# Block-ordered attention steps in a transformer kernel: division at the outputs, weight halves apart, turned q and k through SBUF

## The chip, the cores and the metric

The kernel runs on one core of a Trainium2 chip. The metric is the time of one execution in device microseconds. Three runs of the kernel before gave 3099.89, 3100.74 and 3101.68 us.

## The reference, cut to what matters

The program is two transformer blocks of width 1,024 over 1,024 tokens. The change touches the token mixer of one layer of the second, a "forgetting" attention with 16 heads of 64:

```python
def fox_mixer(h, w_in, b_f, q_g, k_g, w_out):
    proj = h @ w_in
    q, k, v, f_pre = jnp.split(proj, [D, 2 * D, 3 * D], axis=-1)
    q = rms_norm_2(q.reshape(B, S, N_HEADS_2, HEAD_DIM_2), q_g)
    k = rms_norm_2(k.reshape(B, S, N_HEADS_2, HEAD_DIM_2), k_g)
...
    F = jnp.cumsum(log_f, axis=1).transpose(0, 2, 1)
...
        logits = (jnp.einsum('bqhd,bkhd->bhqk', q_i, k).astype(jnp.float32) * scale
                  + (F_i[..., :, None] - F[..., None, :]))
        logits = jnp.where(k_pos[None, :] <= q_pos[:, None], logits, -jnp.inf)
        p = jax.nn.softmax(logits, axis=-1).astype(v.dtype)
        return jnp.einsum('bhqk,bkhd->bqhd', p, v)
...
    return o @ w_out
```

Everything is float32. The kernel splits each operand into a high part in fp32r and the rest, and multiplies high by high, high by low and low by high.

## The kernel before

`attention` works on heads in 8 pairs. For a pair, eight token tiles of 128 are projected: for each tile, 8 slices of k with three matmuls each (`split_mm`, L1622 to L1624) into bank 4. ACT takes q and k out as rows (`rows_out`, L2064) and v in high and low (L2065, with DVE's `v_low`, L2151). Two tiles make a batch: ACT squares, DVE sums (`sums`, L2157), POOL takes the root (`root`, L1907), DVE multiplies (`normed`, L2162), TensorE turns q and k into bank 5 or 6 (`turn_batch`, L2003), and from there ACT writes the high parts (`high_batch`, L2081 to L2083: q once and k twice, for each head) and DVE the low ones (`low_batch`, L2171 and L2173).

A group is 256 query rows of one head, so a pair has 8 groups (4 a head, g = 0 to 3), and a group has g + 1 blocks of 256 keys. For a group: TensorE makes two tiles of logits in banks 0 to 3 (`logits`, L1958 to L1960), DVE adds the forget sums (`forgotten`, L2130), ACT takes the exponential and its row sum (`exp`, L2039), POOL takes the reciprocal and scales the whole rows (`share`, L1912 and L1914), TensorE turns them block by block into bank 5 or 6 (`turn_probs`, L1975), ACT rounds to the high part (`high_probs`, L2048), DVE subtracts (`low_probs`, L2137), and TensorE weighs v (`weigh`, L1991 and L1992) into one half of bank 7. The result has two terms on different partitions: ACT copies one (`copy_out`, L2056) and DVE adds the other (`add_out`, L2144) into `outT`, which is one tile stored per pair by SyncE (L1888).

Every engine's order is written out by hand over slots, one slot for a group. Slot n holds the logits of group n + 1, the turning and weighing of group n, and one whole tile of the next pair's projections, broken up between them. Eight slots ahead of the first group hold the projections of pair 0. `w_qkv` holds half of a pair's weights; a half is loaded by three DMAs (L1864) once DVE has subtracted the one before it (`high_weights`, L2034, and `low_weights`, L2118, both halves in a pair's last slot).

## Time and profile before

| what | value |
| --- | --- |
| median of three runs | 3100.74 us |
| the profiled execution | 3103.1 us, its span 3101.4 us |
| TensorE matmul busy | 2564.8 us, 83% |
| DVE, ACT, POOL busy | 60%, 40%, 18% |
| the stage of the change | from 1548.8 to 2251 us in the span |

Busy shares are over the whole program; the stage of the change is some 702 us of it. A matmul's duration is longer than the distance to the next one's start, since matmuls overlap. Plain rows of a view name the line, the engine, what is written and read, the shape and the count.

### The profile page before, as it was taken

The page shows a single profiled execution, that of the slowest core. Times are in us where ns is not written, and L with a number is a line of the kernel's source. Part 1 is how long each engine was busy: PE and PEld are TensorE (multiplying, and loading weights), DVE is VectorE, ACT ScalarE, POOL GpSimd, SP SyncE. Part 2 cuts the span into 40 slices and gives each one's busy share as a digit, 9 for nine tenths or more (in the row PEclk, how much of TensorE's full clock was granted, in tenths as well). Part 3 has the DMA queues.
Part 4 walks back from the last instruction along what each step waited for, and adds up shares of the span by engine and source line. Part 5 has one row for each costly group of instructions (what it writes and reads, how often), then busy time and mean ns, then how long its engine had stood idle before and what let it go on. Part 6 is the DMA issues. An engine that isn't in the chain of part 4 may idle for free. (4 is left out here: it accounts for less than half of the span.)

```text
span 3101.4 us, 34604 instructions
## 1 busy us (share of the span) xinstructions
PE 2564.8 (83%) x12069; PEld 2116.0 (68%) x12069; DVE 1848.8 (60%) x2460; ACT 1250.9 (40%) x1817; POOL 563.9 (18%) x609
## 2 busy tenths in 40 slices
PE   3998767556999999981478888888685999999999
PEld 2766456455887888870377777777564888888887
DVE  6873693355888888875435555555445445554554
ACT  2212531105777777772245555555422121112111
POOL 1000020111111111104225555555400000000000
PEclk8999758757999999995599999999796999999999
DMA  5683233417968799985111110110042111111111
GB/s 210 220 291 111 96 122 102 158 42 304 393 269 318 289 390 399 398 326 217 55 52 42 41 35 31 41 31 32 7 176 68 41 54 54 41 54 41 54 54 55
DMA packets 137677, 443.01 MB, mean 143 GB/s; under 512 B 15134, under 2 KB 74050, under 8 KB 124264
## 3 DMA queue, kind: packets, MB, share of 16 engines
q1 hardware_dynamic: 124140, 394.97, 34.7%
q0 software_dynamic: 8144, 27.80, 2.5%
q10 hardware_dynamic: 5292, 18.94, 1.5%
q8 instruction: 58, 0.95, 0.1%
q14 instruction: 43, 0.35, 0.0%
HBM read 384.91 MB, written 56.76 MB: 142 GB/s over the span
## 5 line engine op out<-in xcount | busy, mean ns | idle before, releaser
L1622 PE MATMUL psum<-w_high,block_hT_high 128*128 128x512 f32 x576 | 233.4, 405 | 22.8 <-DVE w_low L1328 18.0
L2428 DVE TENSOR_TENSOR x<-x,psum 128x512 f32<-128x512 f32 x256 | 172.8, 685 | 112.4 <-PE psum L1624 112.4
L1622 PE MATMUL psum<-w_qkv_high,fox_hT_high 128*128 128x384 f32 x512 | 199.8, 390 | 34.5 <-DVE w_qkv_low L2118 25.0
L1623 PE MATMUL psum<-w_low,block_hT_high 128*128 128x512 f32 x576 | 226.7, 393 | 0.0
L1624 PE MATMUL psum<-w_high,block_hT_low 128*128 128x512 f32 x576 | 226.4, 393 | 0.0
L1328 DVE TENSOR_TENSOR w_low<-w_up,w_high 128x2048 fp32r<-128x2048 f32 x72 | 161.7, 2288 | 90.0 <-ACT w_high L1322 90.0
L1622 PE MATMUL psum<-hT_high,w_mlp_in_high 128*128 128x512 f32 x512 | 200.1, 391 | 7.1 <-DVE w_mlp_in_low L2405 7.1
L1623 PE MATMUL psum<-hT_low,w_mlp_in_high 128*128 128x512 f32 x512 | 199.9, 390 | 0.0
L1624 PE MATMUL psum<-hT_high,w_mlp_in_low 128*128 128x512 f32 x512 | 199.7, 390 | 0.0
L1622 PE MATMUL psum<-w_mlp_out_high,hiddenT_high 128*128 128x512 f32 x512 | 199.2, 389 | 0.0
L1623 PE MATMUL psum<-w_mlp_out_low,hiddenT_high 128*128 128x512 f32 x512 | 199.2, 389 | 0.0
L1624 PE MATMUL psum<-w_mlp_out_high,hiddenT_low 128*128 128x512 f32 x512 | 199.2, 389 | 0.0
L1328 DVE TENSOR_TENSOR w_low<-w_gate,w_high 128x2048 fp32r<-128x2048 f32 x72 | 164.3, 2284 | 40.0 <-ACT w_high L1322 39.9
L2137 DVE TENSOR_TENSOR probsT_low<-psum,probsT_high 128x512 fp32r<-128x512 f32 (+1 forms) x160 | 98.9, 634 | 135.6 <-ACT probsT_high L2048 135.0
L1623 PE MATMUL psum<-w_qkv_low,fox_hT_high 128*128 128x384 f32 x512 | 176.8, 345 | 0.0
L1624 PE MATMUL psum<-w_qkv_high,fox_hT_low 128*128 128x384 f32 x512 | 176.6, 345 | 0.0
L1322 ACT ACTIVATE w_high<-w_gate 128x2048 fp32r<-128x2048 f32 x72 | 137.5, 1913 | 91.9 <-DMA w_gate<-in_w_expert_gate 84.2
L1991 PE MATMUL psum<-probsT_high,v_high_low 128*128 128x256 f32 x320 | 96.6, 321 | 81.1 <-DVE probsT_low L2137 80.7
L1328 DVE TENSOR_TENSOR w_low<-w_down,w_high 128x2048 fp32r<-128x2048 f32 x72 | 161.5, 2282 | 3.5 <-ACT w_high L1322 3.5
L2416 DVE TENSOR_TENSOR relu_squared<-relu 128x512 f32<-128x512 f32 x64 | 44.2, 691 | 194.2 <-ACT relu L2384 194.2
L2379 ACT ACTIVATE w_mlp_out_high<-w_mlp_out 128x2048 fp32r<-128x2048 f32 x16 | 30.7, 1917 | 319.0 <-DVE w_mlp_out L2409 319.0
L1622 PEld LDWEIGHTS psum<-w_high,block_hT_high 128*128 128x128 f32 x576 | 109.7, 190 | 58.9 <-DVE w_low L1328 32.5
(402 smaller groups left out, 6704.7 us busy)
## 6 DMA issues: line engine op xcount, KB each, us to landing
w_gate<-in_w_expert_gate SPq DMA_DIRECT2D x32, 2048.0 KB
w_up<-in_w_expert_up SPq DMA_DIRECT2D x32, 2048.0 KB, 9.1
w_down<-in_w_expert_down SPq DMA_DIRECT2D x32, 2048.0 KB, 10.4
v_aug<-in_w_ada SPq DMA_DIRECT2D x48, 512.0 KB, 4.8
expert_rows<-block_out ACTq DMA_DIRECT2D x36, 512.0 KB, 9.1
v_aug<-in_ada_w SPq DMA_DIRECT2D x32, 512.0 KB, 4.7
expert_rows<-work SPq DMA_DIRECT2D x1, 16384.0 KB, 44.1
w_mlp_in<-in_w_mlp_in SPq DMA_DIRECT2D x16, 1024.0 KB, 5.1
```

The source lines that it names most:

```text
L1322: act.activation(wh[:, par, half], raw[kind][:, half], ACT.Copy).then_inc(s_wh, 1)
L1328: dve.tensor_tensor(wl[:, par, half], raw[kind][:, half], wh[:, par, half].bitcast(F32), ALU.subtract).then_inc(s_wl, 1)
L1622: pe.matmul(out, sh, mh, start=start, stop=False)
L1623: pe.matmul(out, sh, ml, start=False, stop=False)
L1624: return pe.matmul(out, sl, mh, start=False, stop=stop)
L1991: pe.matmul(out_, v, pTh[:, y % 2, at], start=s == 0, stop=False)
L2137: dve.tensor_tensor(pTl[:, y % 2, 0:width], bank[5 + z % 2][:, 0:width], pTh[:, y % 2, 0:width].bitcast(F32), ALU.subtract).then_inc(s_lo, 1)
L2379: act.activation(w2h[:], w2[:], ACT.Copy).then_inc(s_w2h, 1)
L2416: dve.tensor_tensor(gf[:, g % 2, :], rl[:, g % 2, :], rl[:, g % 2, :], ALU.mult).then_inc(s_sq, 1)
L2428: dve.tensor_tensor(x3[:, t, at], x3[:, t, at], bank[4 + j % 4], ALU.add).then_inc(s_r, 1)
```

## The change

The slots become steps, 20 to a pair, one for each block. Step y turns block y + 1 and weighs block y; a group's logits stand four steps ahead of its first block. The 64 slices of the next pair's projections are dealt to the first 18 steps of a pair (`parts`), and none to the last two. POOL no longer scales the rows: it scales the columns of a diagonal by the reciprocals, a plain f32 matmul of `ones` with it spreads them over the partitions into the second half of bank 7, and DVE multiplies the outputs by that. Bank 7 then holds one group. The two weight halves are rounded at steps 17 and 19 of a pair. Turned q and k are copied by ACT with their gain into the tile of the squares in SBUF; POOL copies the high parts from there, ACT copies k across the partitions, and DVE subtracts in SBUF. The probabilities have a buffer for each g.

```diff
             F = sbuf(c2, "forget_sums", [P, 2, S])
-            pe_ = sbuf(c2, "probs_even", [P, 5 * P + 6 * P])
-            po_ = sbuf(c2, "probs_odd", [P, 7 * P + 8 * P])
+            pb = [sbuf(c2, f"probs{g}", [P, (4 * g + 3) * P]) for g in range(4)]
             pTh = sbuf(c2, "probsT_high", [P, 2, HALF], F32R)
             pTl = sbuf(c2, "probsT_low", [P, 2, HALF], F32R)
             o = sbuf(c2, "outT", [P, S])
+            dg = sbuf(c2, "recip_diagonal", [P, 2, 2 * P])
...
+            STEPS = 20
+            AHEAD = 4
+            BUSY = 18
+            parts = ((0, 4, 8), (0, 4, 8), (0, 3, 6, 8), (0, 4, 8), (0, 4, 8), (0, 3, 6, 8), (0, 4, 8), (0, 4, 8))
+            shares = [(t, range(a_, b_)) for t in range(TT) for a_, b_ in zip(parts[t], parts[t][1:])]
+            blocks = [(n, b) for n in range(NG) for b in range(n % QUADS + 1)]
...
+            def group_at(y):
+
+                n, b = blocks[y + AHEAD] if 0 <= y + AHEAD < NY else (None, 1)
+                return n if b == 0 else None
+
+            def left_at(y):
+
+                n, b = blocks[y - 1] if y >= 1 else (None, None)
+                return n if n is not None and b == n % QUADS else None
+
+            def products_at(y):
+
+                i, c = y // STEPS + 1, y % STEPS
+                if i >= PAIRS or c >= BUSY:
+                    return []
+                t, ks = shares[c]
+                return [(TT * i + t, k) for k in ks]
+
+            def tile_at(y):
+
+                done = [q for q, k in products_at(y) if k == KT - 1]
+                return done[0] if done else None
+
+            def batch_at(y):
+
+                q = tile_at(y) if y >= -STEPS else None
+                return q // 2 if q is not None and q % 2 == 1 else None
+
+            z_block, z_batch = {}, {}
+            for y in steps:
+                if 0 <= y + 1 < NY:
+                    z_block[blocks[y + 1]] = len(z_block) + len(z_batch)
+                if batch_at(y - 2) is not None:
+                    z_batch[batch_at(y - 2)] = len(z_block) + len(z_batch)
+
+            holds = {z: ("block", y_block[nb]) for nb, z in z_block.items()} | {z: ("batch", m) for m, z in z_batch.items()}
...
-                        pool.tensor_scalar(probs(n, u), probs(n, u), rs[:, j % 4:j % 4 + 1], None, ALU.mult).then_inc(s_p, 1)
-
-                    for n in slots:
-                        if batch_in(n) is not None:
-                            root(batch_in(n))
-                        if 0 <= n + 1 < NG:
+                        if n >= 2 and u == 0:
+                            pool.wait_ge(s_rb, n - 1)
+                        pool.tensor_scalar(dg[:, n % 2, u * P:(u + 1) * P], ident[:], rs[:, j % 8:j % 8 + 1], None, ALU.mult).then_inc(s_dg, 1)
+
+                    def high_batch(m):
+                        i, c = divmod(m, 4)
+                        at = slice(2 * c * P, 2 * (c + 1) * P)
+                        pool.wait_ge(s_bs, m + 1)
+                        pool.wait_ge(s_rq, m + 1)
+                        for h in range(2):
+                            pool.tensor_copy(qs[rows[h], i % 2, h, at], sq[rows[h], 0, :])
+                            ins = pool.tensor_copy(kh[rows[h], i % 2, h, at], sq[rows[h], 1, :])
+                        ins.then_inc(s_bh, 1)
+                        pool.wait_ge(s_bh, m + 1)
+
+                    shared = 0
+                    for y in steps:
+                        if batch_at(y - 3) is not None:
+                            if shared:
+                                pool.wait_ge(s_dg, 2 * shared)
+                            high_batch(batch_at(y - 3))
+                        if batch_at(y - 1) is not None:
+                            root(batch_at(y - 1))
+                        if group_at(y - 1) is not None:
                             for u in range(2):
-                                share(2 * (n + 1) + u)
+                                share(2 * group_at(y - 1) + u)
+                            shared += 1
...
+                    def bank_left(z):
+
+                        if z >= 2:
+                            kind, at = holds[z - 2]
+                            if kind == "block":
+                                pe.wait_ge(s_lo, at + 1)
+                            else:
+                                pe.wait_ge(s_bs, at + 1)
+
...
-                            pe.wait_ge(s_p, 2 * n + 2)
+                            pe.wait_ge(s_ex, 2 * n + 2)
...
-                        half = (n % 2) * 2 * P
-                        if b == 0 and n >= 2:
-                            pe.wait_ge(s_o, n - 1)
-                        pe.wait_ge(s_lo, z_block[n, b] + 1)
+                        if b == 0 and n >= 1:
+                            pe.wait_ge(s_o, n)
+                        pe.wait_ge(s_lo, y + 1)
                         for s in (2 * b, 2 * b + 1):
                             v = va[:, i % 2, s, 2 * DH * h:2 * DH * (h + 1)]
                             if s <= 2 * g:
-                                out_, at = bank[7][:, half:half + 2 * P], slice((s % 2) * 2 * P, (s % 2 + 1) * 2 * P)
+                                out_, at = bank[7][:, 0:2 * P], slice((s % 2) * 2 * P, (s % 2 + 1) * 2 * P)
                             else:
-                                out_, at = bank[7][:, half + P:half + 2 * P], slice(2 * P, 3 * P)
+                                out_, at = bank[7][:, P:2 * P], slice(2 * P, 3 * P)
                             pe.matmul(out_, v, pTh[:, y % 2, at], start=s == 0, stop=False)
                             ins = pe.matmul(out_, v, pTl[:, y % 2, at], start=False, stop=s == 2 * g + 1)
                         ins.then_inc(s_pv, 1)
+                        if b == g:
+                            pe.wait_ge(s_dg, 2 * n + 2)
+                            pe.matmul(bank[7][:, 2 * P:HALF], ones[:], dg[:, n % 2, :], start=True, stop=True).then_inc(s_rb, 1)
 
...
-                    for n in slots:
-                        logits(n + 1, 0)
-                        project(n, (0, 1))
-                        logits(n + 1, 1)
-                        project(n, (2, 3))
-                        if n >= 0:
-                            g = n % QUADS
-                            turn_probs(n, 0)
-                            project(n, (4,))
-                            for b in range(g + 1):
-                                if b < g:
-                                    turn_probs(n, b + 1)
-                                    project(n, (5 + b,))
-                                elif g < 3:
-                                    project(n, range(5 + g, KT))
-                                weigh(n, b)
-                        else:
-                            project(n, range(4, KT))
-                        if batch_in(n) is not None:
-                            turn_batch(batch_in(n))
+                    for y in steps:
+                        if 0 <= y + 1 < NY:
+                            turn_probs(*blocks[y + 1])
+                        if group_at(y) is not None:
+                            logits(group_at(y), 0)
+                            logits(group_at(y), 1)
+                        for q, k in products_at(y):
+                            project(q, k)
+                        if y >= 0:
+                            weigh(*blocks[y])
+                        if batch_at(y - 2) is not None:
+                            turn_batch(batch_at(y - 2))
...
-                        act.wait_ge(s_pv, y_block[n, g] + 1)
+                        act.wait_ge(s_rb, n + 1)
                         if g == 0 and h == 0 and i >= 1:
                             act.wait_ge(s_st, 16 * i)
-                        half = (n % 2) * 2 * P
-                        act.activation(o[rows[h], 2 * g * P:2 * (g + 1) * P], bank[7][rows[1 - h], half:half + 2 * P], ACT.Copy).then_inc(s_oc, 1)
-
-                    def rows_out(n):
-                        q = n + TT
+                        act.activation(o[rows[h], 2 * g * P:2 * (g + 1) * P], bank[7][rows[1 - h], 0:2 * P], ACT.Copy).then_inc(s_oc, 1)
+
...
                         act.wait_ge(s_raw, 2 * m + 2)
                         if m >= 1:
-                            act.wait_ge(s_ss, m)
+                            act.wait_ge(s_bh, m)
+                            act.wait_ge(s_bx, m)
+                            act.wait_ge(s_bl, m)
                         act.activation(sq[:], qk[:, 2 * (m % 2):2 * (m % 2) + 2, :], ACT.Square).then_inc(s_sq, 1)
 
...
+                    def stage_batch(m):
+                        z = z_batch[m]
+                        act.wait_ge(s_t, z + 1)
+                        act.wait_ge(s_ss, m + 1)
+                        for x, gain in ((0, gq[:, 2:3]), (1, gq[:, 1:2])):
+                            ins = act.activation(sq[:, x, :], bank[5 + z % 2][:, 2 * x * P:2 * (x + 1) * P], ACT.Copy, scale=gain)
+                        ins.then_inc(s_bs, 1)
                         i, c = divmod(m, 4)
-                        z = z_batch[m]
                         at = slice(2 * c * P, 2 * (c + 1) * P)
-                        src = bank[5 + z % 2]
-                        act.wait_ge(s_t, z + 1)
+                        act.wait_ge(s_bs, m + 1)
                         for h in range(2):
-                            act.activation(qs[rows[h], i % 2, h, at], src[rows[h], 0:2 * P], ACT.Copy, scale=gq[rows[h], 2:3])
-                            act.activation(kh[rows[h], i % 2, h, at], src[rows[h], 2 * P:HALF], ACT.Copy, scale=gq[rows[h], 1:2])
-                            ins = act.activation(kh[rows[1 - h], i % 2, h, at], src[rows[h], 2 * P:HALF], ACT.Copy, scale=gq[rows[h], 1:2])
-                        ins.then_inc(s_hi, 1)
+                            ins = act.activation(kh[rows[1 - h], i % 2, h, at], sq[rows[h], 1, :], ACT.Copy)
+                        ins.then_inc(s_bx, 1)
...
+                    for y in steps:
+                        if 0 <= y + 1 < NY:
+                            high_probs(*blocks[y + 1])
+                        if left_at(y) is not None:
+                            copy_out(left_at(y))
+                        if group_at(y - 1) is not None:
+                            exp(2 * group_at(y - 1))
+                            exp(2 * group_at(y - 1) + 1)
+                        if batch_at(y - 3) is not None:
+                            stage_batch(batch_at(y - 3))
+                        if y % STEPS == BUSY - 1 and y // STEPS + 2 < PAIRS:
+                            high_weights(2 * (y // STEPS + 2))
+                        if tile_at(y) is not None:
+                            rows_out(tile_at(y))
+                        if batch_at(y) is not None:
+                            square(batch_at(y))
+                        if y % STEPS == STEPS - 1 and y // STEPS + 2 < PAIRS:
+                            high_weights(2 * (y // STEPS + 2) + 1)
...
                         dve.wait_ge(s_oc, n + 1)
-                        dve.tensor_tensor(o[rows[h], at], o[rows[h], at], bank[7][rows[h], half:half + 2 * P], ALU.add).then_inc(s_o, 1)
-
-                    def v_low(n):
-                        q = n + TT
+                        dve.tensor_tensor(o[rows[h], at], o[rows[h], at], bank[7][rows[h], 0:2 * P], ALU.add).then_inc(s_oa, 1)
+                        dve.wait_ge(s_oa, n + 1)
+                        dve.tensor_tensor(o[rows[h], at], o[rows[h], at], bank[7][rows[h], 2 * P:HALF], ALU.mult).then_inc(s_o, 1)
...
-                        z = z_batch[m]
                         at = slice(2 * c * P, 2 * (c + 1) * P)
-                        src = bank[5 + z % 2]
-                        dve.wait_ge(s_hi, z + 1)
+                        dve.wait_ge(s_bh, m + 1)
                         for h in range(2):
-                            dve.scalar_tensor_tensor(qs[rows[1 - h], i % 2, h, at], src[rows[h], 0:2 * P], gq[rows[h], 2:3],
-                                                     qs[rows[h], i % 2, h, at].bitcast(F32), ALU.mult, ALU.subtract)
-                            ins = dve.scalar_tensor_tensor(kl[rows[h], i % 2, h, at], src[rows[h], 2 * P:HALF], gq[rows[h], 1:2],
-                                                           kh[rows[h], i % 2, h, at].bitcast(F32), ALU.mult, ALU.subtract)
-                        ins.then_inc(s_lo, 1)
+                            dve.tensor_tensor(qs[rows[1 - h], i % 2, h, at], sq[rows[h], 0, :], qs[rows[h], i % 2, h, at].bitcast(F32), ALU.subtract)
+                            ins = dve.tensor_tensor(kl[rows[h], i % 2, h, at], sq[rows[h], 1, :], kh[rows[h], i % 2, h, at].bitcast(F32), ALU.subtract)
+                        ins.then_inc(s_bl, 1)
...
+                    for y in steps:
+                        if 0 <= y + 1 < NY:
+                            low_probs(*blocks[y + 1])
+                        if left_at(y) is not None:
+                            add_out(left_at(y))
+                        if batch_at(y - 2) is not None:
+                            normed(batch_at(y - 2))
+                        if group_at(y) is not None:
+                            forgotten(2 * group_at(y))
+                            forgotten(2 * group_at(y) + 1)
+                        if batch_at(y - 1) is not None:
+                            sums(batch_at(y - 1))
+                        if batch_at(y - 4) is not None:
+                            low_batch(batch_at(y - 4))
+                        if y % STEPS == BUSY - 1 and y // STEPS + 2 < PAIRS:
+                            low_weights(2 * (y // STEPS + 2))
+                        if tile_at(y) is not None:
+                            v_low(tile_at(y))
+                        if y % STEPS == STEPS - 1 and y // STEPS + 2 < PAIRS:
+                            low_weights(2 * (y // STEPS + 2) + 1)
```

## Rows read from the trace of the kernel before

**Rows 1.** The page's first line.

```profile
span 3101.4 us, 34604 instructions
```

**Rows 2.** Timeline of SyncE's DMA issues: start, duration, line, name, count.

```profile
1693.24 0.50 SPq L1888 DMA_DIRECT2D heads_outputs<-outT  x1
...
2102.43 0.34 SPq L1888 DMA_DIRECT2D heads_outputs<-outT  x1
...
2181.64 69.33 SPq L1888 DMA_DIRECT2D heads_outputs<-outT  x2
```

**Rows 3.** Windows: busy of PE, PEld, DVE, ACT, POOL; granted clock, DMA share, GB/s.

```profile
1857.00:1940.00 83.00, 70.54 (x434) 62.36 (x433) 46.24 (x99) 46.86 (x109) 44.08 (x41) 0.98 0.13 40
2189.00:2251.00 62.00, 41.02 (x189) 32.98 (x187) 25.70 (x53) 23.89 (x52) 30.15 (x24) 0.69 0.00 1
```

**Rows 4.** Waits from 1560 to 2252: total us, times, longest.

```profile
PE psum L1991 <- DVE probsT_low L2137: 80.7, 68, 2.8
```

**Rows 5.** Timeline of TensorE in a middle pair.

```profile
1873.00 0.39 PE L1958 MATMUL psum<-k_high_twice,q_stacked 128*128 128x512 f32 x1
...
1873.96 0.42 PE L1622 MATMUL psum<-w_qkv_high,fox_hT_high 128*128 128x384 f32 x1
...
1874.57 0.33 PE L1622 MATMUL psum<-w_qkv_high,fox_hT_high 128*128 128x384 f32 x1
...
1875.09 0.60 PE L1975 MATMUL psum<-ident,probs_even 128*128 128x128 f32 x4
1875.45 0.42 PE L1622 MATMUL psum<-w_qkv_high,fox_hT_high 128*128 128x384 f32 x1
```

**Rows 6.** Timeline of TensorE, plain f32 matmuls of 512 columns.

```profile
320.46 1.88 PE L549 MATMUL psum<-ucT,wq 128*128 128x512 f32 x4
322.18 1.88 PE L549 MATMUL psum<-ucT,wk 128*128 128x512 f32 x4
```

**Rows 7.** Groups of instructions, 1560 to 2252, shapes kept apart.

```profile
L2137 DVE TENSOR_TENSOR probsT_low<-psum,probsT_high 128x512 fp32r<-128x512 f32 x96 | 64.7, 687 | 77.4 <-ACT probsT_high L2048 77.0
...
L2048 ACT ACTIVATE probsT_high<-psum 128x512 fp32r<-128x512 f32 x96 | 55.0, 589 | 29.6 <-PE psum L1975 29.4
L1907 POOL TENSOR_TENSOR qk_sums<-qk_sums,minus_half 128x8 f32<-128x8 f32 x32 | 53.6, 1674 | 2.7
L1914 POOL TENSOR_SCALAR probs_odd<-probs_odd,row_sum 128x1024 f32<-128x1024 f32 x16 | 45.7, 2854 | 1.6
...
L2171 DVE SCALAR_TENSOR_TENSOR q_stacked<-psum,qk_gain,q_stacked 64x256 fp32r<-64x256 f32 x64 | 30.9, 483 | 48.6 <-ACT k_high_twice L2083 48.2
...
L2081 ACT ACTIVATE q_stacked<-psum,qk_gain 64x256 fp32r<-64x256 f32 x64 | 30.1, 470 | 18.8 <-PE psum L2003 17.5
...
L2144 DVE TENSOR_TENSOR outT<-outT,psum 64x256 f32<-64x256 f32 x64 | 26.7, 417 | 4.1 <-ACT outT L2056 3.2
...
L2056 ACT ACTIVATE outT<-psum 64x256 f32<-64x256 f32 x64 | 24.1, 376 | 19.1 <-PE psum L1992 18.6
...
L2039 ACT ACTIVATE probs_odd<-probs_odd,row_min 128x1024 f32<-128x1024 f32 x16 | 18.4, 1150 | 30.4 <-DVE row_min L2130 30.4
...
L1914 POOL TENSOR_SCALAR probs_even<-probs_even,row_sum 128x256 f32<-128x256 f32 x16 | 14.9, 934 | 1.6
...
L1914 POOL TENSOR_SCALAR probs_even<-probs_even,row_sum 128x128 f32<-128x128 f32 x16 | 9.8, 614 | 1.6
```

**Rows 8.** Timeline of all engines, second weight half of the next pair.

```profile
1600.70 1.76 DVE L2118 TENSOR_TENSOR w_qkv_low<-w_qkv,w_qkv_high 128x1536 fp32r<-128x1536 f32 x1 [1.21 <-ACT w_qkv_high L2034]
...
1604.56 0.66 PE L1622 MATMUL psum<-w_qkv_high,fox_hT_high 128*128 128x384 f32 x1 [3.94 <-DVE v_high_low L2151]
...
1607.51 1.48 ACT L2034 ACTIVATE w_qkv_high<-w_qkv 128x1536 fp32r<-128x1536 f32 x1 [2.85 <-DMA w_qkv<-in_fox_w_in]
```

**Rows 9.** DMA issues, 1540 to 2260: KB each, median us from issue to landing.

```profile
heads_outputs<-outT SPq DMA_DIRECT2D x8, 512.0 KB, 4.8
```

More of the change, by code:

```diff
@@ L2038, in exp @@
                         act.wait_ge(s_add, j + 1)
-                        act.activation(probs(n, u), probs(n, u), ACT.Exp, scale=-1.0, bias=mn[:, j % 4:j % 4 + 1],
-                                       accum_out=rs[:, j % 4:j % 4 + 1]).then_inc(s_ex, 1)
+                        act.activation(probs(n, u), probs(n, u), ACT.Exp, scale=-1.0, bias=mn[:, j % 8:j % 8 + 1],
+                                       accum_out=rs[:, j % 8:j % 8 + 1]).then_inc(s_ex, 1)
                     def high_probs(n, b):
```

126 lines of the change are left out of this document (32 added, 94 removed).

## The prediction

> **What bounds the kernel now.** I read the page first, then stretches by window, then the waits of the attention stage, then its timelines. The change touches one stage, the attention of the second block, from the first projection to the last store of outT. The span is 3101.4 us, and that execution took 3103.1 us, 2.4 us above the median of 3100.7; the sum below is made against 3103.1 and then lowered by 2.4 [rows 1]. Stores of outT go out at 1693.24, 2102.43, 2181.64 and, last, 69.0 us later at 2250.6 (the end of the merged row less its 0.3) [rows 2]: the five pairs in between take 81.8 us each, the next 79.2, the last 69.0. TensorE is busy for 85% of a middle stretch at a granted clock of 0.98, and in the last pair for 66% at 0.69, while DVE, ACT and POOL stay near 55% [rows 3]. No engine is full: the stage is a chain, and 80.7 us of TensorE's idle time end when DVE has written probsT_low [rows 4]. The reader is to see that the probabilities are turned, rounded and weighed within one slot, with too little other work between.
>
> **TensorE's own work in the new order.** A pair has 20 blocks. From start to start [rows 5]: a slice of k takes 0.52, the first behind other work 0.61; four turns 0.36; a 1,024-column logits tile 0.96; four weighing matmuls of 256 columns, at the slices' rate (0.52 for 1,152 columns), 0.46, with the switch 0.5. A pair: 64 slices 33.3 and 18 restarts 1.6; turns 12 x 0.36 + 8 x 0.25 = 6.3; logits 10.0 (9,216 columns a head by that tile's 0.47 ns, and some 0.08 for each of eight tiles); weighing 12 x 0.5 + 8 x 0.4 = 9.2; turned q and k 4 x 0.38 = 1.5. All this is there before too: 61.9. Added: one f32 matmul `ones` x diagonal a group. Plain f32 over 512 columns shows as two records, and four records take 1.72 us [rows 6], so 256 columns take 0.43, with the switch 0.5: 8 x 0.5 = 4.0. New work: 65.9 a pair. Without stalls a pair would save 15.9 us.
>
> **The other engines.** Prices are of [rows 7]. Removed: POOL's scaling of whole rows (0.61 to 2.85 us each); in its place, behind the two reciprocals, two scalings of 128 columns at 0.61 a group. POOL's four new copies of 64x256 a batch are not in the trace: bounds are nothing and 0.93 (the 256-column scaling), I take 0.6, nearer the row; even 3.7 a batch ends before DVE's `low_batch` a step later would start, since that stands behind the forget adds. Cost 0, both ends. ACT's six reads of PSUM at 0.47 become two, and two copies at 0.38: 1.2 less a batch. DVE's four steps go from 0.48 to at most 0.42. Added on DVE: a multiply of 0.42 behind its own add, eight times a pair. ACT and DVE then carry about 45 us a pair: neither bounds by its sum, both do in places.
>
> **Stalls by layout.** I lay out steps 0 to 19: an ACT or DVE instruction with its duration of [rows 7], its engine free about 0.1 before that is over (my reading of ACT and DVE runs), its reader starting 0.03 to 0.1 after.
> First, bank 7 holds one group now, not two. At the eight steps that weigh a group's first block TensorE waits for the group before to be copied, added and multiplied: turn 0.63 to ACT, rounding 0.48, copy 0.40, and on DVE, free at 1.83 behind `low_probs`, add 0.45, multiply 0.42, hand-over 0.12: 2.8 from the step's start. Cover there is 0.36 and the slices (four: 2.53; three: 2.01; two: 1.49) and logits. Steps 3, 10, 11, 6 and 13 lack 0.4, 0.4, 0.6, 0.75 and 1.45: 3.6 a pair.
> Second, at steps 3 and 13 `rows_out` stands behind both exponentials of the widest group (1.15 and a little less) on ACT, so bank 4 comes free 4.9 and 4.6 us after the step began: 1.2 and 1.0 late for steps 4 and 14: 2.2.
> Third, the pair boundary, counted from the start of step 16. DVE does the forget add, `low_batch` (to 8.0), the first weight half at 1.76 (to 9.8), `v_low`, `low_probs` and `sums` (to 11.1); POOL's root with a power of 1.67 ends at 13.2, `normed` at 13.9, so TensorE's turn of the batch, due at 11.4, ends at 14.4: 3.0. The second half's loads can start only at 9.8; in the trace ACT gets them 5.05 us after that point (1602.46 to 1607.51) [rows 8]. ACT rounds them 14.8 to 16.3 at the end of step 19, DVE 16.3 to 18.1, and behind both stand copy, add and multiply of the old pair's last group: to 19.6, while TensorE is ready at 16.9: 2.6. The store of outT leaves then and lands 4.8 us later [rows 9]; `copy_out` of the next pair's first group waits for it at step 1, with `rows_out` queued behind: its weighing starts at 25.8 instead of 22.9: 2.9. With 0.3 at step 2: 8.8.
> Sum: 65.9 + 3.6 + 2.2 + 8.8 = 80.5. TensorE is idle for about half of 18 us at the boundary, and after 3.94 us of waiting the trace shows a 384-column matmul at 0.66 [rows 8], the level of 1.2 GHz. Cost between nothing and the doubled work of steps 20 to 22 that no wait hides (4); I take 1.1 as the waits for DMA hide most. A pair: 81.6 against 81.8.
>
> **The sum.** Head: the projections of pair 0 keep their gaps; the first store needs no wait for an earlier store (-3.6) and meets the same boundary once: 1690.8 against 1693.24: -2.4. Five pairs: 5 x (81.6 - 81.8) = -1. Pair 6 has no weight loads at its boundary: 77.6 against 79.2: -1.6. Last pair, no projections to cover: 2.9 (3.1 at the lower clock) plus weighing at each of the eight group starts, 1.35 to 1.45 at each block within a group (turn, round, subtract, weigh, two in flight), 8 for logits: about 62 against 69.0, since POOL's 2.85 has left the chain: -7. Total -12: 3103.1 - 12 = 3091.1, on the scale of the median 3089.
>
> **One rule against the change.** Row-scaling on POOL keeps one price for equal widths although DVE's two-input subtractions run beside it, 1.76 for the weight half too [rows 7, 8], so the sum has no contention. The Trainium skill, GPSIMD Engine Reference, its table at the head, has the SBUF interfaces of GpSimd shared with VectorE, with contention when VectorE has two SBUF inputs. `low_batch` becomes such an instruction: by the rule up to its 1.4 us would be added four times a pair.
>
> **The rivals.**
> (1) The boundary is met with other work and its waits overlap. If all 8.8 went, six boundaries give back 53 and the time is 3036; half gone, 3063. For it: the three waits are one chain, and one link arriving earlier shortens all. Against it: load, store and root have rows.
> (2) Slower, one mechanism: the boundary leaves TensorE at 1.2 GHz and steps 20 to 22 run doubled. Four to five us at each of seven boundaries instead of 1.1: 3089 + 7 x 3.4 = 3113. It decides once a boundary loses more than 2.5 us beyond the layout. For it: the low clock after one 3.94 us gap, and 0.69 in the last pair. Against it: middle pairs hold 0.98 through waits of 2.6.
> (3) No change: the waits for probsT_low only trade places with those for bank 7, and the last pair stays at 69: 3096 to 3100.
> (4) Contention on the shared interface, worked out as a mechanism: 1.4 x 4 a pair, of which at most half reaches TensorE, 2.8 x 7 = 20: 3109. The page named above has it; the rows show none.
>
> **How the numbers follow.** My layout, about 3075 to 3100: 0.5 (of it 0.32 faster, 0.16 same, 0.02 slower); rival 1: 0.22; rival 2: 0.2; rival 3: 0.05; rival 4: 0.03. A measurement of this kernel tells about 0.2%, 6 us, from no change. Faster 0.54, same 0.21, slower 0.25. The range reaches to half of rival 1 and past rival 2: 3057 to 3116; the likeliest case's own is 3075 to 3103.
>
> **What would show it.** Waits for probsT_low nearly gone from the weighing; new waits of TensorE for outT at group starts, some 0.3 to 1.5 each; ACT's outT waiting for the store and w_qkv_high for a DMA once a pair; the f32 matmul as two records of about 0.21 apart; stores 80 to 83 apart, the last one 60 to 64. Wrong if the stores lie 76 or 85 apart: then the boundary is mis-sized, by overlap or by the clock.

## The result and the profile after

The changed kernel takes 3109.65 us (median of 7 runs, 3104.45 to 3115.11), the kernel before 3101.27 (7 runs): ratio 1.0026, 95% interval 1.0015 to 1.0038. It is slower by 0.26%, on the other side from the forecast of 3089, inside the range. Names and lines are those of the changed kernel: `turn_probs` L2030, `weigh` L2045 and L2046, the matmul of `ones` L2050, `turn_batch` L2058, `high_weights` L2081, `copy_out` L2102, `add_out` L2188 and L2190, `root` L1941, `share` L1946 and L1950, the store of outT L1922.

The page's first line, and the stores of outT in SyncE's timeline (start, duration, line, name, count), which answer to [rows 1, 2]:

```profile
span 3109.1 us, 35143 instructions
```

```profile
1697.22 0.50 SPq L1922 DMA_DIRECT2D heads_outputs<-outT  x1
...
1782.78 0.50 SPq L1922 DMA_DIRECT2D heads_outputs<-outT  x1
...
2124.15 0.34 SPq L1922 DMA_DIRECT2D heads_outputs<-outT  x1
...
2202.81 54.75 SPq L1922 DMA_DIRECT2D heads_outputs<-outT  x2
```

Read as in [rows 2], the last store starts at 2257.24. This execution took 3110.87 us. Against 3091.1 forecast for it:

| stretch | before | forecast | after | after less forecast |
| --- | --- | --- | --- | --- |
| first store | 1693.24 | 1690.8 | 1697.22 | +6.4 |
| five pairs | 5 x 81.8 | 5 x 81.6 | 5 x 85.4 | +18.9 |
| pair 6 | 79.2 | 77.6 | 78.7 | +1.1 |
| last pair | 69.0 | 62 | 54.4 | -7.6 |
| after the last store | 850.8 | 850.8 | 851.9 | +1.1 |

The loss is in the middle pairs. Windows of one middle pair and of the last pair, columns as in [rows 3]:

```profile
1860.00:1946.00 86.00, 74.88 (x440) 67.62 (x440) 47.39 (x102) 42.04 (x98) 32.43 (x57) 0.92 0.12 36
...
2203.00:2257.24 54.24, 37.23 (x203) 30.23 (x203) 27.49 (x58) 23.30 (x52) 15.39 (x28) 0.82 0.03 11
```

The middle pair shown holds the slowest boundary of the run: its clock is 0.92. From store to store the clock is 0.94 in each of the five middle pairs, where it was 0.98 in four of the five. In the last pair it is 0.82 where it was 0.69; over the whole stage it is 0.94 in both kernels. Waits of the stage, from 1560 to 2258 (total us, times, longest), which answer to [rows 4]:

```profile
PE psum L2045 <- DVE outT L2190: 48.9, 39, 2.8
...
POOL recip_diagonal L1950 <- PE psum L2050: 43.0, 9, 5.8
...
DVE qk_rows L2207 <- POOL qk_sums L1941: 29.4, 18, 2.1
PE psum L2058 <- DVE qk_rows L2207: 27.9, 16, 3.5
ACT w_qkv_high L2081 <- DMA w_qkv<-in_fox_w_in: 26.4, 7, 4.1
...
ACT outT L2102 <- DMA heads_outputs<-outT: 14.8, 6, 3.0
...
PE psum L2045 <- DVE probsT_low L2182: 3.9, 10, 0.5
```

The wait for probsT_low fell from 80.7 to 3.9, and the ones forecast have come: outT, the store, the weights' DMA. One that the prediction does not have stands among them: POOL's scaling of the diagonal waits 43.0 for the matmul of `ones`. Groups of the stage, shapes apart (busy, mean ns of one), for [rows 7]:

```profile
L2050 PE MATMUL psum<-recip_diagonal,ones 128*128 128x256 f32 x128 | 41.9, 409 | 0.0
...
L2215 DVE TENSOR_TENSOR k_low<-qk_square,k_high_twice 64x256 fp32r<-64x256 f32 x64 | 28.2, 440 | 0.9
L2214 DVE TENSOR_TENSOR q_stacked<-qk_square,q_stacked 64x256 fp32r<-64x256 f32 x64 | 26.9, 420 | 3.4 <-POOL k_high_twice L1959 2.0
L2190 DVE TENSOR_TENSOR outT<-outT,psum 64x256 f32<-64x256 f32 x64 | 26.8, 418 | 2.2
...
L1959 POOL CAST k_high_twice<-qk_square 64x256 fp32r<-64x256 f32 x64 | 25.5, 398 | 0.0
L1958 POOL CAST q_stacked<-qk_square 64x256 fp32r<-64x256 f32 x64 | 25.3, 395 | 123.1 <-ACT qk_square L2126 81.0 <-issue 40.7
```

The new instructions cost what the prediction took or less: the multiply 0.42, the casts 0.40 against 0.6. So a price was not the fault. I then cut the pairs at the starts of the turns (L2030), which gives the length of each step. Means over the five middle pairs stand beside the layout behind the prediction. Of that layout only the prices, the stalls and the sums are on record; the lengths of single steps are mine, and adding up the recorded prices and stalls step by step gives each of them to about 0.15. The column adds to 80.4, without the 1.1 for the clock:

| step | layout | after | third diagonal buffer | three edits |
| --- | --- | --- | --- | --- |
| 0 | 6.0 | 5.84 | 6.07 | 5.28 |
| 1 | 5.85 | 5.96 | 6.01 | 2.89 |
| 2 | 5.55 | 7.38 | 7.09 | 6.61 |
| 3 | 3.4 | 3.36 | 3.35 | 2.99 |
| 6 | 3.4 | 3.36 | 3.36 | 2.64 |
| 10 | 4.2 | 5.57 | 4.21 | 3.84 |
| 11 | 3.0 | 3.16 | 3.15 | 2.38 |
| 13 | 3.45 | 3.51 | 3.50 | 2.53 |
| 14 | 3.95 | 4.49 | 3.91 | 4.80 |
| 19 | 6.1 | 6.59 | 6.48 | 6.54 |
| other ten | 35.5 | 36.16 | 36.17 | 35.99 |
| pair | 80.4 | 85.38 | 83.31 | 76.49 |

Sixteen steps are within 0.2 us of the layout. Four are not: 10, 2, 14 and 19. The last two columns are runs told below. Timeline of step 10, all engines:

```profile
1902.43 0.57 POOL L1946 TENSOR_TENSOR row_sum<-row_sum,minus_one 128x1 f32<-128x1 f32 x1 [0.93 <-ACT probs L2086]
...
1906.93 0.68 DVE L2202 TENSOR_REDUCE qk_sums<-qk_square 128x8 f32<-128x512 f32 x1
...
1908.01 0.65 PE L2050 MATMUL psum<-recip_diagonal,ones 128*128 128x256 f32 x2
...
1908.84 0.61 POOL L1950 TENSOR_SCALAR recip_diagonal<-ident,row_sum 128x128 f32<-128x128 f32 x1 [5.84 <-PE psum L2050]
...
1911.06 1.67 POOL L1941 TENSOR_TENSOR qk_sums<-qk_sums,minus_half 128x8 f32<-128x8 f32 x1
...
1912.76 0.69 DVE L2207 TENSOR_TENSOR qk_rows<-qk_rows,qk_sums 128x512 f32<-128x512 f32 x1 [1.54 <-POOL qk_sums L1941]
...
1913.60 0.63 PE L2058 MATMUL psum<-ident,qk_rows 128*128 128x128 f32 x4 [1.17 <-DVE qk_rows L2207]
```

The diagonal has two buffers, so `share` of a group may not write before the matmul of `ones` has read the diagonal of the group two before it (`wait_ge(s_rb, n - 1)`). `share` runs three steps ahead of its group's first block, which is step 11 here. The group two before ends only with step 9, because the group between them has a single block. So POOL has stood idle for 5.84 us when it may write. `root` is behind `share` on POOL although its sums are ready at 1907.6, so `normed` and `turn_batch` are late and TensorE stands 1.17.

### The profile page after: what moved, and what is told of

Its sections match the earlier page's. It is cut to its first block and busy times, and to the rows that moved or that the text cites. A ratio compares the mean times of both kernels' runs of the same rounds, so it can differ in the third digit from the quotient of the medians.

```text
span 3109.1 us, 35143 instructions
## 1 busy us (share of the span) xinstructions
PE 2584.5 (83%) x12197; PEld 2142.9 (69%) x12197; DVE 1868.7 (60%) x2524; ACT 1220.0 (39%) x1753; POOL 473.7 (15%) x737
## 5 line engine op out<-in xcount | busy, mean ns | idle before, releaser
L1622 PE MATMUL psum<-w_qkv_high,fox_hT_high 128*128 128x384 f32 x512 | 192.1, 375 | 43.5 <-DVE w_qkv_low L2163 24.2
L2095 ACT ACTIVATE probsT_high<-psum 128x512 fp32r<-128x512 f32 (+1 forms) x160 | 88.4, 552 | 263.3 <-PE psum L2030 263.1
```

What stands on the lines that cost most here:

```text
L1622: pe.matmul(out, sh, mh, start=start, stop=False)
L2095: act.activation(pTh[:, y % 2, 0:width], bank[5 + z % 2][:, 0:width], ACT.Copy).then_inc(s_hi, 1)
```

## The experiments

Ratios are to the kernel before, measured beside each. The changed kernel itself was not run again beside them, so gains on it are differences to its 3109.65. "Pair" is the mean of the five middle spacings.

**The clock at the boundary (e1_awake).** Turns of the identity, which write what is later overwritten, fill TensorE's waits at the boundary.

```diff
+                        if m % 4 == 3:
+                            for _ in range(24):
+                                pe.transpose(bank[5 + z % 2][:, 0:P], ident[:], ident[:])
                         pe.wait_ge(s_qn, m + 1)
...
+                        if 0 <= y < NY - STEPS and y % STEPS in (0, 1):
+                            pe.wait_ge(s_add, 2 * (8 * (y // STEPS) + 2) + 2)
+                            for _ in range(8 if y % STEPS == 0 else 24):
+                                pe.transpose(bank[0][:, 0:P], ident[:], ident[:])
                         if y >= 0:
                             weigh(*blocks[y])
```

> The changed kernel with idle turns of the identity on TensorE inside its three waits at each pair boundary (24 before the turn of the pair's last batch, 8 before the first weighing of step 0, 24 before that of step 1, into banks that nobody reads then). Clock theory (the boundary's pauses drop TensorE to 1.2 GHz and steps 20 to 22 run at that level, 4 us a pair): matmuls behind the boundary stay at the short distances, stores of outT 81 to 83 us apart instead of 85.4, 3085 to 3095 us in all. Wait theory (the boundary is only longer in its waits for loads and stores, the clock is a bystander): no gain, 3108 to 3115.

3118.37 us (4 runs), ratio 1.0069 (1.0052 to 1.0086), above both expectations; pairs of 85.6. The stage's mean granted clock rose from 0.94 to 0.97, and step 2 runs at the level of 2.4 GHz in six of the seven pairs (5.39 to 6.43), where the changed kernel has 6.41 to 9.13. First the changed kernel (the 512-column matmul of step 2 of a pair in TensorE's timeline), then this run:

```profile
1873.22 0.38 PE L2045 MATMUL psum<-probsT_high,v_high_low 128*128 128x256 f32 x1 [2.42 <-DVE outT L2190]
...
1875.17 0.77 PE L2006 MATMUL psum<-k_high_twice,q_stacked 128*128 128x512 f32 x1 [0.76 <-DVE k_low L2215]
1875.73 0.63 PE L2007 MATMUL psum<-k_low,q_stacked 128*128 128x512 f32 x1
```

```profile
1873.05 0.39 PE L2045 MATMUL psum<-probsT_high,v_high_low 128*128 128x256 f32 x1 [0.80 <-DVE outT L2197]
...
1874.99 0.47 PE L2006 MATMUL psum<-k_high_twice,q_stacked 128*128 128x512 f32 x1 [0.77 <-DVE k_low L2222]
1875.30 0.39 PE L2007 MATMUL psum<-k_low,q_stacked 128*128 128x512 f32 x1
```

The mean clock was restored and the time was not. What was expected of rival 2 is refuted as the main cause. The fillers lengthen step 1 in some pairs (up to 7.1), and the profiled execution (3109.59) is the fastest of the four, so this run alone does not show that the clock costs nothing.

**The store of outT (e2_split_store).** Each head's rows are stored by themselves, so the first group of a pair waits for a store issued more than 40 us earlier.

```diff
                         if i + 1 < PAIRS:
                             forget(i + 1, 0)
+                        sp.wait_ge(s_o, 8 * i + 4)
+                        sp.dma_start(o_dram[i * P:i * P + DH, :], o[rows[0], :]).then_inc(s_st[0], 16)
+                        if i + 1 < PAIRS:
                             forget(i + 1, 1)
...
-                        sp.dma_start(o_dram[i * P:(i + 1) * P, :], o[:]).then_inc(s_st, 16)
+                        sp.dma_start(o_dram[i * P + DH:(i + 1) * P, :], o[rows[1], :]).then_inc(s_st[1], 16)
...
-                        if g == 0 and h == 0 and i >= 1:
-                            act.wait_ge(s_st, 16 * i)
+                        if g == 0 and i >= 1:
+                            act.wait_ge(s_st[h], 16 * i)
```

> The changed kernel with outT stored in two halves, head 0's rows as soon as its four groups are through, head 1's at the end, so that the first copy of the next pair waits for a store long landed. Wait theory alone: 2.4 to 2.9 us less at each of six boundaries, 3092 to 3096. Clock theory on top of it: a shorter pause also shortens the slow stretch, 4 to 6 us less a boundary, 3075 to 3088.

3094.44 us, ratio 0.9977 (0.9962 to 0.9992), where the wait theory put it. Step 1 falls from 5.91 to 3.01 (medians), as the 2.9 of the prediction has it. Step 2 falls from 7.38 to 6.49 in the mean: with the wait of step 1 gone, all seven boundaries keep 2.4 GHz in step 2 (6.33 to 6.60), where the changed kernel has 6.41 to 9.13. So here lies a clock cost of 0.9 a pair that goes with the wait. Step 14 is still slow in three pairs (5.31 to 5.46).

**The weights' load (e3_two_w) and both (e4_both).** A second buffer for `w_qkv`, so that a half loads while the one before is rounded. To make room, the forget sums keep one buffer: the kernel leaves out those of the second head, so its result is wrong, and it has one load a pair less.

```diff
-            F = sbuf(c2, "forget_sums", [P, 2, S])
+            F = sbuf(c2, "forget_sums", [P, 1, S])
-            w = sbuf(c2, "w_qkv", [P, KT // 2, W3])
+            ww = [sbuf(c2, "w_qkv0", [P, KT // 2, W3]), sbuf(c2, "w_qkv1", [P, KT // 2, W3])]
...
-                        if m >= 1:
-                            sp.wait_ge(s_wl, m)
+                        if m >= 2:
+                            sp.wait_ge(s_wl, m - 1)
```

> The changed kernel with two tiles for loaded weight halves, so that no load waits for a subtraction. To make room head 1 uses the forget sums of head 0, a changed result, with one load of them less a pair. Wait theory: ACT's 26.4 us of waits for loads vanish, and the first weighing of step 0 comes 2 to 2.6 us earlier, 3092 to 3098. Clock theory: 4 to 6 us less a boundary, 3070 to 3086, with TensorE at the short distances in more of steps 20 to 22.

3088.66 us, ratio 0.9965 (0.9955 to 0.9975); pairs of 82.2. That lies between the two expected ranges. Step 0 falls by 0.5, from 5.84 to 5.34, and step 1 by 2.3, from 5.96 to 3.66, though the edit does not touch the store that step 1 waits for.

> Both edits together (and head 1 with head 0's forget sums). Wait theory: the two add, about 5.5 us a boundary, 3070 to 3078. Clock theory: what is left of the pause (the root and the batch, 3 us) is too short to drop the clock, so about 9 us a boundary, 3045 to 3060, stores 75 to 78 apart.

3082.0 us, ratio 0.9947 (0.993 to 0.9965); pairs of 81.6, and again neither of the expected ranges. Alone the two edits gain 15.2 and 21.0 on the changed kernel, together 27.7 and not 36.2: load and store are links of one chain, and an earlier load takes most of the wait for the store with it (2.3 of 2.9). Rival 1's mechanism is there, but the changed kernel does not have the overlap by itself. The load that these two runs lack was not tested alone.

**The finished group first (e5_first).** ACT copies a finished group before it rounds the next block, and DVE adds and multiplies before it subtracts. The edit on ACT (that on DVE moves `add_out` in the same way):

```diff
+                        if left_at(y) is not None:
+                            copy_out(left_at(y))
                         if 0 <= y + 1 < NY:
                             high_probs(*blocks[y + 1])
-                        if left_at(y) is not None:
-                            copy_out(left_at(y))
```

> The changed kernel with the copy and the add of a finished group ahead of the rounding and the subtraction of the next block, on ACT and on DVE. The layout puts 3.6 us a pair on TensorE's waits for bank 7 at steps 3, 6, 10, 11 and 13; this order has the result out 1.1 us sooner: 3 to 4 us less a pair and 3 to 6 in the last pair, 3075 to 3088. Rival (bank 7 is not what holds steps, the rounding that now comes later is): within 4 us of the changed kernel, 3106 to 3114.

3094.99 us, ratio 0.9974 (0.9963 to 0.9984), between the two expected ranges. Steps 3, 6, 11 and 13 fall to 2.99, 2.64, 2.37 and 2.52, but step 2 rises to 8.4 to 9.0 in five of seven pairs and step 14 to 6.0 to 6.1 in four, where the slices run at 1.2 GHz. The last pair takes 46.5 instead of 54.4.

**The rows ahead of the exponentials (e6_rows_first).**

```diff
+                        early = y % STEPS in (3, 13) and tile_at(y) is not None
+                        if early:
+                            rows_out(tile_at(y))
                         if group_at(y - 1) is not None:
                             exp(2 * group_at(y - 1))
...
-                        if tile_at(y) is not None:
+                        if tile_at(y) is not None and not early:
                             rows_out(tile_at(y))
```

> The changed kernel with ACT's copies of the projected rows ahead of the exponentials at steps 3 and 13. Layout: bank 4 free 1 to 1.2 us sooner, twice a pair, 2 us a pair, 3092 to 3098. Rival (the exponentials then come late for their turns): no gain or 1 us a pair worse, 3108 to 3120.

3106.37 us, ratio 1.0015 (1.0003 to 1.0026), an interval that overlaps the changed kernel's. Step 4 falls from 3.69 to 2.46 and step 14 to 2.91, without one slow step 14 in seven; step 5 rises from 3.34 to 5.21, since the exponentials end later. The wait has moved by one step.

**The division left out (e7_before_noscale, e8_nodiv).** In the kernel before, POOL's scaling of the rows goes; in the changed one the matmul of `ones`, the multiply and the wait of POOL for them.

```diff
-                        pool.tensor_scalar(probs(n, u), probs(n, u), rs[:, j % 4:j % 4 + 1], None, ALU.mult).then_inc(s_p, 1)
...
-                            pe.wait_ge(s_p, 2 * n + 2)
+                            pe.wait_ge(s_rc, 2 * n + 2)
```

```diff
-                        if n >= 2 and u == 0:
-                            pool.wait_ge(s_rb, n - 1)
...
-                            pe.matmul(bank[7][:, 2 * P:HALF], ones[:], dg[:, n % 2, :], start=True, stop=True).then_inc(s_rb, 1)
...
-                        dve.tensor_tensor(o[rows[h], at], o[rows[h], at], bank[7][rows[h], 2 * P:HALF], ALU.mult).then_inc(s_o, 1)
```

> The kernel before without POOL's scaling of the rows (the reciprocals stay; the outputs come undivided). If the last pair's gain (54.4 us after, 69.0 before) comes from the scaling having left the chain: last pair 55 to 60 us, the middle pairs little changed, 3085 to 3095. Rival (the gain comes from the order by blocks): last pair 66 to 69, 3097 to 3101.

> The changed kernel without the f32 matmul with ones and the multiply (the outputs come undivided; reciprocals and diagonals stay). By the layout: 0.5 us of TensorE and 0.45 of DVE's chain for each of 64 groups, 5 to 7 us a pair as both stand in the wait for bank 7: 3055 to 3075. Rival (they hide in waits): 3095 to 3110.

e7 takes 3100.13 us, ratio 0.9996 (0.9986 to 1.0007), in the range of its rival; its last pair takes 63.6 instead of 69.0, in neither of the ranges expected for it. e8 takes 3068.76 (4 runs), ratio 0.9895 (0.9874 to 0.9916), as expected, with pairs of 80.5, step 10 at 3.52 and a last pair of 48.6. Both outputs come undivided; the reciprocals stay in both, the diagonals in e8. Side by side: without the division the new order is 31 us faster than the old one; the division costs 1 to 2 us at its old place, not clear of noise, and 41 at its new one.

**A third diagonal buffer (e9_ring3).**

```diff
-            dg = sbuf(c2, "recip_diagonal", [P, 2, 2 * P])
+            dg = sbuf(c2, "recip_diagonal", [P, 3, 2 * P])
...
-                        if n >= 2 and u == 0:
-                            pool.wait_ge(s_rb, n - 1)
+                        if n >= 3 and u == 0:
+                            pool.wait_ge(s_rb, n - 2)
...
```

> The changed kernel with a third buffer for the diagonal; nothing else differs. The theory that the lost 1.4 us at step 10 come from GpSimd (its scaling of the diagonal waits for the ones-matmul of two groups before, with root queued behind it) expects step 10 to go from 5.57 to about 4.2 us, GpSimd's wait of 43.0 us at the scaling to be gone, and the middle pairs to be 84.0 us instead of 85.4: 3109.6 - 7 x 1.4 = about 3100. The rival that turn_batch is late for another reason at step 10 (normed stands behind other work of DVE) expects no change, 3107 to 3111.

3101.34 us (11 runs), ratio 0.9995 (0.9982 to 1.0007): 8 us off the changed kernel, about the 3100 expected. Step 10 is 4.21, as in the layout, in all seven pairs. POOL and DVE at that step:

```profile
1886.60 0.61 POOL L1950 TENSOR_SCALAR recip_diagonal<-ident,row_sum 128x128 f32<-128x128 f32 x1
...
1890.23 1.67 POOL L1941 TENSOR_TENSOR qk_sums<-qk_sums,minus_half 128x8 f32<-128x8 f32 x1
...
1893.40 0.68 DVE L2207 TENSOR_TENSOR qk_rows<-qk_rows,qk_sums 128x512 f32<-128x512 f32 x1
...
1894.53 0.60 PE L2058 MATMUL psum<-ident,qk_rows 128*128 128x128 f32 x4
```

`share` ends at 1887.2, the power of `root` starts 0.4 after the sums are there, and neither `normed` nor `turn_batch` waits. Step 14 is 3.91 in all seven pairs of this execution; that is not shown to be the third buffer's doing, since the next run has it too and is slow there in five of seven. The profiled execution (3086.95) is the fastest of the eleven, so its pairs of 83.3 flatter the edit by some of the 14 us between it and the median; the step lengths do not depend on that.

**Edits together (e10_ring_split, e12_ring_split_first, e11_all_ring).** The edits are those above; the last one also has the rows ahead of the exponentials and rounds the second weight half behind the copy and add of the next step.

> The third buffer for the diagonal together with the store of outT split in two halves by head (3094.4 alone). If the two losses lie at different places of a pair they add up: 3094.4 - 9 = about 3085, pairs of 81.4 us. The rival is that one covers the other: about 3094.

3082.92 us, ratio 0.9949 (0.9932 to 0.9965): the two add up as expected (15.2 + 8.3 = 23.5; measured 26.7). Step 14 takes 5.38 to 5.48 in five of the seven pairs.

> Third buffer, split store, and ACT's copy and DVE's add and multiply of a finished group ahead of the next block's rounding (3095.0 alone, with 2.9 us more at the steps 2 and 14 and about 2.9 less over the steps 3, 6, 11 and 13). If the three add up: 3109.6 - 9.5 - 15 - 14.6 = about 3070. The rival, that the earlier copy now delays the turned probabilities at every group's start and gains only in the last pair (8 us there): about 3077.

3049.01 us, ratio 0.9836 (0.9815 to 0.9857), 21 us below what was expected. Alone, the earlier copy gained 14.7; on top of the other two it gains 33.9. Stage and last stores of this run (columns as above):

```profile
1560.00:2194.34 634.34, 562.41 (x3508) 517.33 (x3508) 378.40 (x815) 329.80 (x784) 265.62 (x448) 0.97 0.13 36
```

```profile
2112.37 0.45 SPq L1918 DMA_DIRECT2D heads_outputs<-outT  x1
2149.05 0.45 SPq L1925 DMA_DIRECT2D heads_outputs<-outT  x1
2175.26 0.45 SPq L1918 DMA_DIRECT2D heads_outputs<-outT  x1
2194.34 0.45 SPq L1925 DMA_DIRECT2D heads_outputs<-outT  x1
```

The same matmuls (3,508 and 3,506 records) keep TensorE busy for 562.4 us here and 591.4 in the changed kernel, at a mean clock of 0.97 and 0.94. Alone the earlier copy had been paid for in slow matmuls, step 2 at 8.4 to 9.0, and in a wait for the store (step 1 at 6.5 in the mean). Here step 1 is 2.89, step 2 is 6.20 to 6.77 in all seven pairs, and step 14 is slow in one. The last pair takes 45.3.

> As the run with three edits, and the rows of a tile copied ahead of the exponentials at steps 3 and 13 (3106.4 alone, -3.3), and the second weight half rounded a step later, behind the copy and add of the step that begins a pair. If the wait for the weights' DMA at the boundary (26.4 us in all, 7 times) goes with no new wait, 3070 - 3 - 6 x 2 = about 3055. The rival, that the boundary is held by the chain of root, normed and turn_batch whatever the weights do, expects 3067 to 3077.

3048.82 us, ratio 0.9831 (0.9808 to 0.9854): the same as the run before, and below both expectations, which had started from 3070. The two further edits bring nothing: step 14 falls to 3.04 and step 4 to 2.82, but step 5 rises to 5.20 and step 15 to 4.41, and at the boundary steps 19 and 0 stay (6.58 and 5.39 against 6.54 and 5.28). That fits the rival's reason, that load and rounding of the weights no longer hold the boundary.

## Why the prediction was wrong

**The steps that failed** are two: "Cost 0, both ends" for POOL, in "The other engines", and the third part of "Stalls by layout" with the clock term behind it. The prediction had a middle pair at 81.6 and got 85.4, five times. Its sign of being wrong, stores 85 apart, came, but it laid that to the boundary alone. Of these 3.9 above the layout's 81.5:

- 1.37 at step 10. The prediction never listed what waits behind `share` on POOL. It priced `share` (two scalings of 0.61) and gave POOL "cost 0, both ends", having looked at durations alone and not at the new wait for the matmul of `ones`. Shown by the third buffer: 5.57 to 4.21.
- 0.9 at step 2, at full clock (6.41 instead of 5.55). The logits of the widest group wait for `low_batch`, which stands behind the add and multiply on DVE (1872.75, then 1873.19 to 1874.9, TensorE at 1875.17). I had 0.3 for it. At full clock it stays at 6.2 to 6.9 in the five middle pairs of every run that keeps the division, so no run removed it: read from the timeline, not tested.
- 0.4 more for the clock than the 1.1: 0.97 at step 2 and 0.54 at step 14. Step 14 I had not named: behind waits of 1.28 and 0.79 its four slices run mostly at 1.2 GHz in three of the seven pairs, 5.4 instead of 3.9. What decides that is open.
- 0.5 at step 19, part of it two pairs with 6.84, its cause not sought; and 1.0 in twelve steps of 0.02 to 0.16 each.

These make 4.2, and steps 0, 3, 6 and 8 give 0.3 back. Only the first is a whole mechanism that was missing, and the only one whose removal alone was measured. Without it the pairs would stand at 84.0, still above the 81.8 of before: mis-sizings of the boundary and of the clock did most of the rest. So of the 3.9, 1.37 is shown by an edit, the clock's part at step 2 goes away with the wait for the store (e2), and the rest is read from step lengths.

**The head** came 6.4 late. From the second turn to the first store, steps 10, 2, 14 and 19 again add 1.4 + 0.9 + 1.5 + 0.3; most of the other 2.3 lies ahead of them, and I can't name it.

**The last pair** took 54.4, not 62, and it was wrong in its sum and in its reason. The sum first. A group's start takes 3.35 to 4.79, the eight together 30.4; the blocks within groups and the logits take the other 24.0, where the prediction had 12 x 1.4 + 8 = 24.8. Two blocks within a group take 2.7 together, 1.37 each, as forecast. The logits do cost their time, for in steps 2 and 12 TensorE works without a wait from the turn to the weighing:

```profile
2208.51 1.05 PE L2030 MATMUL psum<-ident,probs 128*128 128x128 f32 x4
2209.56 0.76 PE L2006 MATMUL psum<-k_high_twice,q_stacked 128*128 128x512 f32 x1
...
2212.75 0.36 PE L2045 MATMUL psum<-probsT_high,v_high_low 128*128 128x256 f32 x1
...
2219.81 0.60 PE L2030 MATMUL psum<-ident,probs 128*128 128x128 f32 x4
2220.17 0.30 PE L2006 MATMUL psum<-k_high_twice,q_stacked 128*128 128x128 f32 x1
...
2222.59 0.38 PE L2045 MATMUL psum<-probsT_high,v_high_low 128*128 128x256 f32 x1 [1.57 <-DVE outT L2190]
```

Only the 0.85 of logits at 2220.17 lies in the shadow of a wait for outT. So the group starts were mis-sized: 62 leaves 37.2 for them, 4.65 each, and they took 3.8 each. The terms as printed do not give 62 either: 3.1 plus a weighing of 0.5, or 0.95 at the lower clock, makes 54 to 57 in all. Now the reason. The prediction had the gain of 7 come from POOL's scaling leaving the chain. e7 and e8 show another account: POOL's scaling had cost 5.4 there (69.0 to 63.6), the division at its new place costs 5.8 (48.6 to 54.4), and the order by blocks gains 15.0 (63.6 to 48.6). The two places of the division cancel, and the gain is the order.

**Right:** the waits for bank 7 (steps 3, 6, 11 and 13 within 0.16), those behind the exponentials (steps 4 and 14 at full clock within 0.1), the store's 2.9, the wait of ACT for the weights' DMA, TensorE's new work. All of the stalls that were laid out came where they were laid. Pair 6 came 1.1 late, with the same 1.37 at step 10 in it.

**The rivals.** Rival 4 gave the nearest time, 3109, by luck: its mechanism, contention, took 3.5 us of POOL's time where 20 was asked for, and it is not on the path (see below). Rival 2 came next (3113) for a cause that isn't the main one: at steps 2 and 14 the clock costs about 1.5 a pair, not 4 to 5. Rival 1 is refuted for this kernel and shown for an edited one. Rival 3 is refuted: the last pair fell to 54.4.

**The rule weighed.** The rows of the kernel before said less than the prediction took from them. Its weight subtractions of 1.76 never ran beside an instruction of POOL, and the other subtractions read one of their two large operands from PSUM. After the change the casts take 0.395 to 0.398 and `low_batch` 0.420 and 0.440 a piece, so 2.8 a pair did not come. But a slowing is there, where `low_batch` reads two tiles of SBUF while POOL works. All engines, at the end of step 17 of a pair:

```profile
1770.23 0.42 DVE L2215 TENSOR_TENSOR k_low<-qk_square,k_high_twice 64x256 fp32r<-64x256 f32 x1
...
1770.66 0.42 DVE L2214 TENSOR_TENSOR q_stacked<-qk_square,q_stacked 64x256 fp32r<-64x256 f32 x1
...
1770.73 0.82 POOL L1950 TENSOR_SCALAR recip_diagonal<-ident,row_sum 128x128 f32<-128x128 f32 x1
...
1771.09 0.50 DVE L2215 TENSOR_TENSOR k_low<-qk_square,k_high_twice 64x256 fp32r<-64x256 f32 x1
```

POOL's scaling takes 0.82 instead of 0.61, DVE's subtraction 0.50 instead of 0.42. The Trainium skill, GPSIMD Engine Reference, section Specifications, says that GpSimd and VectorE share SBUF interfaces and contend when VectorE has two SBUF inputs. The trace agrees in kind: 16 of the 128 scalings are slow (0.77 to 0.85), each beside two or more instructions of `low_batch`. Over the stage the 128 average 637 ns, 27 more than 0.61 or 3.5 us in all. Fourteen of the slow ones lie in steps 7 and 17, which take 4.07 in all pairs, against 4.03 by the prediction's prices, so they cost TensorE next to nothing. `normed` reads two tiles of SBUF too, one of them eight values wide, and POOL's instructions beside it keep 0.55 and 0.61.

## What to carry to other kernels

When a change adds a wait, list for each engine what stands behind the waiting instruction, the cheap engines too: here a wait of POOL that costs POOL nothing held a root that TensorE needed. A ring of buffers has to be as deep as the shortest items that pass through it, not the mean ones. Leaving out a whole feature on both sides (the division, before and after) told at once which half of a change pays, 31 us, and which half costs, 41. Of the 41 the third buffer gives back 8; how the rest divides between the matmul of `ones` and the multiply was not tested. An edit that shortens one wait can be worth little alone, if another wait or slow matmuls take its place, and more in company: the earlier copy gained 14.7 alone and 33.9 on top of two others.

## What the runs showed of the hardware

- The granted clock is not decided by one wait alone. Step 14 of the changed kernel stands behind the same waits in every pair (1.28, then 0.79 or 0.78), and its slices run at 0.52 in one pair and at 0.33 in the next. Over the runs with these two waits it is slow in none (e9) to five (e10) of seven pairs:

```profile
1755.11 0.66 PE L1622 MATMUL psum<-w_qkv_high,fox_hT_high 128*128 128x384 f32 x1 [0.79 <-ACT qk_rows L2109]
...
1756.21 0.52 PE L1622 MATMUL psum<-w_qkv_high,fox_hT_high 128*128 128x384 f32 x1
...
1840.63 0.41 PE L1622 MATMUL psum<-w_qkv_high,fox_hT_high 128*128 128x384 f32 x1 [0.78 <-ACT qk_rows L2109]
...
1841.23 0.33 PE L1622 MATMUL psum<-w_qkv_high,fox_hT_high 128*128 128x384 f32 x1
```

- A plain f32 matmul of 256 columns shows as two records and holds TensorE for 0.49 us (1908.01 to the next turn at 1908.50), as the prediction took it.
